# A prefetch hint on the branch that closes TensorE's job loop

## What is computed

```python
    h = rmsnorm(x, norm_mix)
    proj = h @ w_in                                   # queries, latents, keys, values, gates
    y_mla = mla_attention(...)
    y_diff = diff_attention(...)
    merged = g_mla * (y_mla @ w_up_mla) + g_diff * (y_diff @ w_up_diff)
    x = x + merged @ w_out
    t = rmsnorm(x, norm_ffn)
    top_val, top_idx = lax.top_k(t @ w_router + b_router, 4)
    # per expert e and its rows xb:
    act = clamped_swiglu(xb @ w1[e] + b1[e])          # 1024 -> 2048 -> 1024
    y = act @ w2[e] + b2[e]                           # weighted, added to x at the token
    return rmsnorm(x, norm_final)
```

## Time and profile before

| | us |
|---|---|
| median of three runs | 3142.17 |
| lowest and highest | 3139.12, 3142.42 |
| the profiled execution | 3134.34 |
| its span in the profile | 3132.9 |
| TensorE busy in the span (matmuls) | 2802.6, 89% |
| idle ahead of L1769 | 123.1 |

### The profile page before, as it was taken

How to read it: one execution, slowest core, us unless ns; L and a number is a source line. 1 busy time by engine, 2 the same in 40 slices (tenths; PEclk the granted TensorE clock), 3 DMA queues, 4 the chain that set the end, 5 groups by cost and what they waited for, 6 DMA issues and landing times. The chain is left out here.

```text
span 3132.9 us, 42305 instructions
## 1 busy us (share of the span) xinstructions
PE 2802.6 (89%) x15008; PEld 2249.7 (72%) x15009; DVE 1380.4 (44%) x2316; ACT 858.8 (27%) x1378; POOL 281.5 (9%) x316
## 2 busy tenths in 40 slices
PE   6988888887999997998888988888899999999993
PEld 3346654444666554787788878788799999999992
DVE  4345444447111136332233333344466666666663
ACT  2024332225111011121122222222234344444443
POOL 0000000000000113000000000000111111111111
PEclk9989788898999996998899999999999999999996
DMA  4000000001111444555566656667899999999993
GB/s 123 1 10 4 4 14 14 13 13 40 41 40 40 146 88 120 198 173 158 158 183 183 192 176 205 190 208 220 263 302 339 343 342 341 341 341 343 341 315 129
DMA packets 425325, 524.24 MB, mean 167 GB/s; under 512 B 29332, under 2 KB 336184, under 8 KB 425160
## 3 DMA queue, kind: packets, MB, share of 16 engines
q1 hardware_dynamic: 401256, 459.85, 45.5%
q0 software_dynamic: 19584, 61.39, 8.3%
q10 hardware_dynamic: 4352, 0.98, 0.2%
HBM read 482.23 MB, written 39.95 MB: 167 GB/s over the span
## 5 line engine op out<-in xcount | busy, mean ns | idle before, releaser
L1769 PE MATMUL banks<-arena 128*128 128x128 f32 (+8 forms) x8448 | 1163.8, 301 | 123.1 <-issue 122.0
L1769 PEld LDWEIGHTS banks<-arena 128*128 128x128 f32 x8448 | 1141.1, 194 | 148.9 <-issue 128.9
L1880 DVE TENSOR_SCALAR arena<-banks,arena 128x256 f32<-128x256 f32 x528 | 230.8, 479 | 739.3 <-PE banks L1769 739.2
L1794 PE MATMUL banks<-parts 128*128 128x512 f32 x2160 | 498.5, 391 | 0.0
L1794 PEld LDWEIGHTS banks<-parts 128*128 128x128 f32 x2160 | 403.0, 188 | 82.4
L1868 DVE TENSOR_TENSOR parts<-arena,parts 128x1024 fp32r<-128x1024 f32 x264 | 312.8, 1222 | 94.0 <-ACT parts L1832 92.4
L1832 ACT ACTIVATE parts<-arena 128x1024 fp32r<-128x1024 f32 x264 | 264.8, 1048 | 52.5 <-PE banks L1794 52.5
L1841 ACT ACTIVATE arena<-arena 128x512 f32<-128x512 f32 x132 | 83.2, 630 | 478.1 <-DVE arena L1880 478.1
L1843 ACT ACTIVATE parts<-arena 128x512 fp32r<-128x512 f32 x132 | 83.3, 631 | 468.7 <-DVE arena L1888 442.8
L1125 PE MATMUL banks<-parts 128*128 128x512 f32 x768 | 185.9, 402 | 4.3 <-DVE parts L1189 4.3
L1125 PEld LDWEIGHTS banks<-parts 128*128 128x128 f32 x768 | 146.2, 191 | 41.9 <-issue 12.2
(11 more groups left out here) (267 smaller groups left out, 2417.5 us busy)
## 6 DMA issues: line engine op xcount, KB each, us to landing
arena<-in_w SPq DMA_DIRECT2D x264, 1024.0 KB, 7.6
arena<-in_w SPq DMA_DIRECT2D x66, 2048.0 KB
arena<-in_w_in SPq DMA_DIRECT2D x27, 512.0 KB, 5.1
arena<-in_x SPq DMA_DIRECT2D x16, 512.0 KB, 3.9
h_rows<-arena POOLq DMA_DIRECT2D x10, 512.0 KB, 7.8
acc_rows<-arena SPq DMA_DIRECT2D x8, 512.0 KB, 3.0
out<-arena POOLq DMA_DIRECT2D x8, 512.0 KB, 3.3
arena<-acc_rows SPq DMA_DIRECT2D x1, 3072.0 KB, 13.9
```

The lines of the kernel that those rows point to most:

```text
L1769: last = nc.tensor.matmul(bank(g, 2 * (c % 2) + s)[:, a * JOB:a * JOB + width], w1[c][:, s, k, a * P:(a + 1) * P], xt[:, k, 0:width], star ...
L1794: last = nc.tensor.matmul(bank(g, 2 * h + c), x[:, f, rows], pieces[q][:, y, a, :], start=(f == 0 and x is act_hi and y == 0), stop=(f == ...
L1880: nc.vector.tensor_scalar(dst[:, a * JOB:(a + 1) * JOB], bank(g, 2 * (c % 2) + s)[:, a * JOB:(a + 1) * JOB], b1_t[:, bass.ds(expert, 1), s ...
```

## The change

The loop is opened by another call. It runs on the same engine, over the same range, with the same body. With `hint_back_edge=True` the builder puts one instruction at the head of each pass, ahead of everything else in it: a branch prefetch hint, which names the loop's closing branch and says that it will be taken. The closing branch itself and the rest of the program stay.

```diff
@@ -1809,7 +1809,7 @@
             pe.wait_ge(gathered, 32)
             turn_x(2)
             total = pe.value_load(g.total[0:1, 0:1], min_val=EXPERTS, max_val=JOBS)
-            with pe.Fori(0, JOBS) as n:
+            with nc.Fori(0, JOBS, engines=[mybir.EngineType.PE], hint_back_edge=True) as n:
                 with pe.If(total > n):
                     count = pe.value_load(g.job_count[0:1, bass.ds(n, 1)], min_val=0, max_val=SEQ)
                     next_count = pe.value_load(g.job_count[0:1, bass.ds(n + 1, 1)], min_val=0, max_val=SEQ)
```

## The result

The changed kernel takes 3052.6 us (median of four runs, 3050.7 to 3059.0) against 3142.3 before: a ratio of 0.9722, 95% interval 0.9706 to 0.9738. The forecast was 3094.8 within 3075 to 3160. The sign and the place were right, the size was not: 47.4 us were forecast, 89.7 came (3142.3 less 3052.6). Run again beside other kernels on one chip it measured 0.9748 (0.9726 to 0.977).

The account below looks back on a forecast made before the run. TensorE, 89% busy, was the bound, with 122.0 us idle in code-fetch gaps. Steps 11.2, first returns 18.9, second return 13.8 and narrow return 5.5 gave 49.4, less 2.0 issue: 47.4 us less, 3094.8 us; overall range 3075 to 3160.

Parts of the forecast that it names:

- E+1: Code block after the loop's end, fetched in sequence but never executed; the hint was to stop that fetch.
- H: Code block with the loop's head; fetched 0.46 us sooner with the hint, 1.6 us less per closing branch that misses.
- The store of eight blocks: TensorE's code store bounded at seven or eight blocks; the forecast took eight, enough for a repeated width with the hint.
- H sooner only: Rival: with seven blocks or another replacement order, 12 closing branches gain 1.6 us each; 17 us less, 3125; chance 0.13.
- a ring: The code store keeps the last eight blocks or so; nine in fixed order push each out just before its return.
- E: Code block holding the loop's end with its closing branch, entered by a long jump from every wide body.
- H+1: Code block behind the loop's head, one of the nine packets fetched when a width repeats.
- The repeats: Gaps where a wide width returns: 6.3 us less at first returns to 240, 192, 176; 13.8 at the second to 240.
- The steps: Seven gaps where the width steps down: only the closing branch gains, 1.6 us each, 11.2 us less.
- the closing branch also hits in some steps: Lower end of the forecast's range, 3075: the loop's closing branch needs no fetch, 4.6 us each, four of them 18.
- The first narrow return: Gap at the first return from 128 to 128: the head's block is not pushed out, 5.5 us less.
- Still larger gains, if H is kept for good: Outcome of the head's block never leaving the code store; counted within the forecast's chance of 0.35.

Follow-up runs that it names:

- The 192 body: Changed kernel's hint with three widths (128, 192, 256) in place of nine; 12.5 us idle in 3 gaps, against 81.0 in 8 without the hint.
- the padded body: Changed kernel with 128 never-executed transposes (256 instructions) added to each body above width 128; 92.0 us idle in 13 gaps, 113 packets.
- the kernel without any gap: Kernel of before with the loop's end copied into each body and a hint for it at the body's start; 2990.8 us, ratio 0.9518.

## Why the prediction was right and wrong

**What bounds the kernel and what the hint does: right.** The gap ahead of L1769 was where the time went; with the hint one packet of each return is gone, the one read as E+1, and the closing branch fell to 2.9 to 3.4 us (3.2 forecast). That the hint put H in the place of E+1 is the reading that fits all runs. The two experiments that put another instruction at the head or the hint at the tail left both numbers where they were.

**The store of eight blocks: right in size, wrong in the order of replacement.** Eight was the upper end of seven or eight, and H sooner only (3125 us) was the rival for seven. The 192 body closes with eight and the padded body opens with nine. But the picture of a ring that "keeps the last eight blocks or so" does not hold. The code queue of the changed kernel over the 208 body (1665 to 1731 us), and over the return behind it (1731 to 1741.4):

```profile
q8 instruction: 3, 0.05, 0.3%
```

```profile
q8 instruction: 3, 0.05, 1.7%
```

E, H and H+1 were fetched in the return before (1655.1 to 1661.7), the body fetched three more, and all three are fetched again (1732.7 to 1738.8): six blocks in a pass, so a store that keeps the last eight fetched would still have held them. A reading that fits: a fetched block takes the place in the ring behind the block being executed, whatever stands there, and not the place of the oldest. The body's three new blocks then fall on E, H and H+1. Followed block by block, this gives the returns that fetch and those that do not, in the changed kernel and in the one with the loop's end beside the head, where the first returns to 192 and 176 fetch two blocks although seven would fit. No run was made to test it.

**The repeats: near.** The second return to 240 gave 13.8 us as forecast. The three first returns were put at 6.3 each and gave 7.7 to 8.1 (13.98 to 6.24, 13.65 to 5.88, 13.82 to 5.69), 4.7 us more together. The dispatch branch explains little of it: it had cost 4.94, 5.35 and 5.20 us there, and the sum took 4.94 for each, 0.7 too little in all. Most of the rest lies in the 1.6 us for a closing branch that misses, which left out that H+1 comes sooner too; the padded kernel gives 2.5 us for it.

**The steps: the term that was mis-sized.** They were put at 1.6 us each, seven times, 11.2, with the reason that "H has been pushed out by the new body's blocks". That is so when H was loaded and three new blocks followed. But at a step that follows a repeat nothing has been fetched since the return before it: over the third 240 job and the step behind it (1511 to 1590 us) the view of DMA has no row for the code queue at all. The repeated body ran from the store, E and H were both in it, and the step's target too. The blocks of the new body only push H out for the return after. So three of the seven steps close completely, 8.96 + 8.37 + 8.72 = 26.1 us where 4.8 were forecast. The other four gave 1.7 to 2.7 each, 8.8 in all for 6.4. The steps together: 34.9, not 11.2. The timeline of after shows it in the row at 1586.26, which has no bracket. The forecast's own range named "the closing branch also hits in some steps", but priced it at 4.6 us in four steps, the branch alone, and not the whole gap that goes when nothing has to be fetched.

**The first narrow return: too much.** 5.5 was forecast, 1.4 came (5.50 to 4.06). The closing branch still takes 4.9 us there (6.5 before), with one code packet in it (2180.8 us) where before had two (2263.1 and 2264.7). So E+1 is gone here too, but H still had to be fetched: by the same reading the blocks of the narrow body had taken its place before E was entered.

**The clock: a term that was missing.** A job that follows a gap can start at a lower granted clock. Before, job 3, after 13.98 us idle; then job 4 of the changed kernel, with no gap (columns: stretch, length, busy and count of each engine, PEclk, DMA share, GB/s):

```profile
1442.30:1449.30 7.00, 6.98 (x21) 6.08 (x22) 0.00 (x0) 0.00 (x0) 2.91 (x3) 0.62 0.47 134
```

```profile
1510.80:1517.80 7.00, 7.00 (x36) 6.58 (x36) 0.12 (x1) 1.97 (x2) 3.40 (x3) 1.00 0.30 40
```

In 7 us the first issues 21 matmuls at a granted clock of 0.62, the second 36 at 1.00: a mix of the levels 1.2 and 2.4 GHz after an idle engine, 2.4 throughout after a busy one. With no gap the 256 matmuls of a 240 job take 52.10 us. Behind one they take up to 2.8 more, but not in proportion to its length: 54.73 us after 13.98 idle, 53.51 after 6.24, and 54.84 after 3.35; in the run padded with no-operations it was 52.10 after 3.20 and 54.90 after 6.15. Over the group of L1769 the matmuls took 8.1 us less than before, and 26.6 less (1137.2 us) in the kernel without any gap. The forecast priced a gap by its length alone.

**The sum again, on the profiled executions.** Steps 34.9, first returns to 240, 192 and 176 23.6, second return to 240 13.8, first narrow return 1.4, first job 0.1: 73.9 of idle time, where the forecast had 49.4 before issue. Matmuls at a higher clock 8.1. The hint's issue is 0.035 us each and shows nowhere (2.0 was set aside for it). Together 82.0 of the 83.4 us that the spans differ by; 0.7 of the rest lies ahead of the experts. The median fell by 6 us more than the profiled execution, which before had been 8.0 below its median.

**The range.** The time lies below it. "Still larger gains, if H is kept for good" had a part of the forecast's chance, but the range began at 3075, which is 67 us below the median of before, while 122.0 us of gaps stood in the trace. The two terms that fell short, 23.7 us of the steps and 8.1 of the clock, are what took the time below it; by the steps alone it would have stood at about 3071. No row set a floor under the gaps that the hint could close, so the low end rested on the walk through the steps alone, and that walk was the wrong one.

## What to carry to other kernels

A loop whose pass touches more code than the engine's store holds pays at its branches, and the profile shows it where no wait does: idle time with "issue" as releaser, branches of 3 to 6 us on the sequencer's lines, and packets on the code queue inside the gap. Count the blocks that one pass touches, the one fetched ahead of each jump included; one block too many made all nine of a repeat miss here, so a change that takes one away can be worth the whole gap, and its effect has to be walked through the store in the order of the jobs. A hint at the head of the pass worked and one just ahead of its branch did not; where the loop's end can lie beside the head, or in each body with a hint of its own, that gains more (0.9608 and 0.9518 here, for 0.9748 of the changed kernel on the same chip).

## What the runs showed of the hardware beyond what was expected

The hint costs 0.031 to 0.055 us of the sequencer. One packet fewer is moved in a return, so it seems to replace the sequential prefetch rather than add to it. Never-executed code counts: 256 instructions that are jumped over took a place in the store, which cost 43.9 us of idle time (92.0 for 48.1) and 11.3 us of slower matmuls behind it (1167.0 for 1155.7 in the group of L1769). 256 no-operations in the same place changed nothing (69 packets, 45.3 us). A block fetched three packets earlier can be gone while eight fit: E, H and H+1 were fetched again in every return of the changed kernel from a body above width 128 that had itself fetched three. And the clock after a gap is part of the gap's price: 52.1 us for 256 matmuls without a gap, up to 54.9 behind one, whether it was of 3 us or of 14.
